# The low-part rotary matmul of the attention scores over all 128 contraction rows

## What is computed

```python
sc = jnp.einsum("bqhd,bkhd->bhqk", q_blk.astype(jnp.float32), k_all) * scale
p = jax.nn.softmax(sc, axis=-1)
```

## Time and profile before

| | us |
|---|---|
| median of 3 runs | 2900.56 |
| lowest and highest | 2898.85, 2903.95 |
| profiled execution, first to last instruction (span) | 2900.2 |
| TensorE busy in it | 2776.2 (96%) |
| VectorE, ScalarE, GpSimd busy | 1664.2, 854.4, 384.8 |

### The profile page before, as it was taken

One profiled execution on the slowest core, in us unless ns is written; L12 is line 12 of the kernel. 1 busy time (PEld: TensorE's weight loads), 2 busy tenths in 40 slices (PEclk: granted clock), 3 DMA queues, 4 the chain that ended last, 5 costly groups with the idle time before them and its releaser, 6 DMA issues.

```text
span 2900.2 us, 31209 instructions
## 1 busy us (share of the span) xinstructions
PE 2776.2 (96%) x11986; PEld 2134.7 (74%) x11986; DVE 1664.2 (57%) x1770; ACT 854.4 (29%) x1102; POOL 384.8 (13%) x266
## 2 busy tenths in 40 slices
PE   6889999999899999999999899999999999999996
PEld 6656777777685888888888766664758888888884
DVE  5635656566526654545444689997275444444455
ACT  2223444444424222222222242224342222222221
POOL 0302122222202440404130010000010000000001
PEclk9989999999998999999999999999989999999998
DMA  6201111111332331313121210110321111111112
GB/s 245 96 17 40 44 40 47 36 51 38 108 112 89 108 109 43 101 58 101 57 81 51 94 73 30 30 43 1 116 77 47 44 58 43 51 51 43 51 41 111
DMA packets 55063, 193.96 MB, mean 67 GB/s; under 512 B 5840, under 2 KB 7120, under 8 KB 54992
## 3 DMA queue, kind: packets, MB, share of 16 engines
q1 hardware_dynamic: 28048, 99.07, 10.5%
q10 hardware_dynamic: 15424, 51.98, 4.7%
q0 software_dynamic: 11520, 41.95, 4.5%
HBM read 172.00 MB, written 20.97 MB: 67 GB/s over the span
## 4 chain that ended last, share of the span: by engine, by line
PE 90%; DVE 4%; issue 3%; ACT 1%; DMA 1%; POOL 0%; ACTq 0%; POOLq 0%; SPq 0%; DVEq 0%
PE psum L1227 25%; PE psum L1229 24%; PE psum L1228 24%; PE psum L1577 4%; PE psum L1439 3%; PE psum L1437 3%; PE psum L1248 2%; PE psum L1449 2%; PE psum L1235 1%; DVE f32r_region L797 1%; PE psum L1281 1%; DMA f_region<-ctx_t 1%; PE psum L1288 1%; PE psum L1424 0%; DVE f_region L801 0%
## 5 line engine op out<-in xcount | busy, mean ns | idle before, releaser
L1227 PE MATMUL psum<-f32r_region 128*128 128x512 f32 (+1 forms) x3288 | 1302.3, 396 | 48.0 <-DVE f32r_region L797 13.2
L1229 PE MATMUL psum<-f32r_region 128*128 128x512 f32 (+1 forms) x3288 | 1273.8, 387 | 0.0
L1228 PE MATMUL psum<-f32r_region 128*128 128x512 f32 (+1 forms) x3288 | 1273.7, 387 | 0.0
L1227 PEld LDWEIGHTS psum<-f32r_region 128*128 128x128 f32 x3288 | 625.8, 190 | 191.1 <-issue 32.8
L1228 PEld LDWEIGHTS psum<-f32r_region 128*128 128x128 f32 x3288 | 626.6, 191 | 126.0 <-issue 6.0
L1229 PEld LDWEIGHTS psum<-f32r_region 128*128 128x128 f32 x3288 | 625.2, 190 | 127.0
L384 ACT ACTIVATE f32r_region<-f_region 128x1024 fp32r<-128x1024 f32 (+1 forms) x251 | 254.4, 1024 | 497.3 <-PE psum L1229 446.9
L1095 DVE SCALAR_TENSOR_TENSOR f_region<-psum,vectors,f_region 128x1023 f32<-128x1023 f32 x88 | 112.8, 1282 | 492.4 <-ACT f_region L673 492.4
L673 ACT ACTIVATE f_region<-psum,vectors 128x1024 f32<-128x1024 f32 x88 | 106.2, 1207 | 589.4 <-PE psum L1229 589.4
L1112 DVE TENSOR_TENSOR f_region<-f_region,psum 128x1024 f32<-128x1024 f32 x160 | 194.8, 1217 | 146.4 <-PE psum L1229 146.4
L347 POOL TENSOR_TENSOR f_region<-f_region,f32r_region_plain 128x512 f32<-128x512 f32 x32 | 52.8, 1649 | 1530.5 <-DVE f_region L1055 1530.5
(11 more groups left out here) (108 smaller groups left out, 1891.1 us busy)
## 6 DMA issues: line engine op xcount, KB each, us to landing
f_region<-units SPq DMA_DIRECT2D x178, 512.0 KB, 3.5
f_region<-mod_w POOLq DMA_DIRECT2D x80, 512.0 KB, 3.9
residual<-f_region ACTq DMA_DIRECT2D x24, 512.0 KB, 4.9
f32r_region_plain<-residual ACTq DMA_DIRECT2D x24, 512.0 KB, 7.7
f32r_region_plain<-mod_w ACTq DMA_DIRECT2D x8, 1024.0 KB, 16.5
f_region<-x_t SPq DMA_DIRECT2D x4, 1024.0 KB, 28.0
heads_out<-f_region ACTq DMA_DIRECT2D x16, 256.0 KB, 2.0
f_region<-heads_out ACTq DMA_DIRECT2D x8, 512.0 KB, 4.3
```

Source lines behind the costliest of these rows:

```text
L1227: pe.matmul(out, wl, xh, start=first, stop=False)
L1228: pe.matmul(out, wh, xl, start=False, stop=False)
L1229: return pe.matmul(out, wh, xh, start=False, stop=last)
```

## The change

The matmul of query high by key low no longer takes rows 0 to 63 of its two operands but all 128. Rows 64 to 127 add the product of query low by key low, which was left out before. Order, tiles, semaphores and columns are the same. In the changed file the last matmul moves up one line, from L1439 to L1438.

```diff
                     three(PS[:, at:at + width], [r(R_Q + p * L + q, P) for p in range(2)],
                           [r(KS[(par // 2) % 2] + p * KEYS + at, width) for p in range(2)], True, False)
 
-                    pe.matmul(PS[:, at:at + width], r(R_Q + 2 * L + q, P)[:ROPE], r(R_KR + KEYS + at, width)[:ROPE],
-                              start=False, stop=False)
+                    pe.matmul(PS[:, at:at + width], r(R_Q + 2 * L + q, P), r(R_KR + KEYS + at, width), start=False, stop=False)
                     mm = pe.matmul(PS[:, at:at + width], r(R_Q + 2 * L + q, P), r(R_KR + at, width), start=False, stop=True)
```

## The result

| | before | after |
|---|---|---|
| median of the runs, us | 2899.7 (4 runs) | 2819.15 (4 runs) |
| lowest and highest, us | 2898.73, 2903.95 | 2816.7, 2822.91 |
| span of the profiled execution, us | 2900.2 | 2819.3 |

The ratio is 0.9717, 95% interval 0.9705 to 0.9729: 2.8% less time. Set against the 2900.56 us from which the prediction started, that is 2818.5 us. Each run of the changed kernel is 1.8 us longer than its span (2821.07 us for the profiled one), so the two profiles compare span with span: 80.9 us.

What follows compares the result with a forecast made beforehand. TensorE was taken to bound the attention scores. From the 2900.2 us span, 76.8 us for row changes came off and 3 us for new waits went back on: 2826.4 us, given as 2826, range 2819 to 2840 us.

Steps and rivals of the forecast that it cites:

- The bound: Attention scores, 197 to 766 us: TensorE sets the time, busy 560.73 of 569 us, VectorE 339.08, ScalarE 223.10.
- The price of a change: Score blocks: about 0.2 us for each switch between 128 and 64 rows, 1.20 us per score step, 76.8 us in all.
- The second way: Idle times before the weight loads of L1437 and L1439, 47.6 + 32.0 = 79.6 us; 80 kept as upper end.
- That a full-height matmul at this place is not stalled: At L1437, 128 rows would fall back to starts 0.23 us apart, so the full 76.8 us is gained.
- the argument from the one-row matmuls: Line 1255: eight one-row matmuls in a row take 1.05 us without stalling, so few rows are not slow in themselves.
- The allowance for new waits: Score steps where VectorE's row maximum comes late: 0 to 12 us of the gain lost, 3 us in the sum.
- VectorE's reserve: VectorE's wait for the scores before the row maximum (L925) falls from 145.5 to about 70 us.
- The clock: Attention stage: mean granted clock read as 0.98 of 2.4 GHz; a microsecond allowed for it in the range.
- VectorE's chain: Rival, score steps: VectorE late by 1.2 us in a quarter to half of 64 steps, 19 to 38 us back; chance 0.06.
- one stall staying: Rival, score blocks: the load of L1439 stays held, half of 76.8 us remains, 2862 us; chance 0.04.
- nothing happening: Rival, score blocks: the hole belongs to the place or the instruction's shape costs nothing, 2900 us; chance 0.03.
- a price by rows: Rival, L1437: the stall grows with rows loaded, 0.2 us for 64 and 0.4 for 128, 2939 us; chance 0.02.

Runs made afterwards that it cites:

- grouped: Kernel before with the three 64-row matmuls of a score step run one after another at its end, not one in each block: 2837.41 us, ratio 0.9782.
- doubled 64-row matmuls: Kernel before with the last matmul of each score block also cut to 64 rows, so two stand in a row: 2900.43 us, ratio 0.9997.
- the late steps: Changed kernel with 64 rows in the low-part rotary matmul in the last 8 of 64 score steps only: 2832.96 us, ratio 0.9759.

## Why the prediction came out as it did

The direction and the mechanism were right. The size was short: 2826 us was forecast, and the median of 2819.15 us is at the lower end of the range, by the ratio (2818.5 us) half a microsecond outside it. That half microsecond is within the noise of the whole time (the interval is 2815 to 2822 us); the stage, which repeats to 0.3 us, shows the errors behind it. Step by step:

- *The bound.* TensorE sets the stage, and 79.7 of the 80.9 us came out of it. Right.
- *The price of a change.* 1.20 us a step from the starts, 76.8 us in all. The score blocks gave 76.6. Right. The second way, 79.6 us of idle time before the loads, agreed by luck. The 129 waits of each load are, but for one, those of the 128 wide blocks, 0.37 and 0.25 us and so 0.62 us a block where the starts give 0.41, and the idle times before the loads of the narrow blocks, 0.14 and 0.13 us or 16.6 us in all, are too short for that view. So 80, the upper end, was no bound.
- *That a full-height matmul at this place is not stalled.* Right, and the argument from the one-row matmuls, that a run of low matmuls is not slow and only the change is, is what the kernels with grouped and with doubled 64-row matmuls showed.
- *The allowance for new waits, 3 us, up to 12.* This step failed: nearly nothing of it came. TensorE's wait for the exponential went from 6.4 to 6.8 us; the steps with a late maximum had their cover, and VectorE's reserve shrank as forecast (70 us, 70.2 measured). The reserve held, but for half a microsecond in one early wait, even with a further 34.7 us taken out of the stage.
- *The clock.* This step failed too, and it is the one that carries the time past the range: without the 3 us for waits, 2900.2 - 76.8 is 2823.4 us, still inside. The sum had no term for the clock and the range gave it one microsecond; what stands in the places with a lowered clock is 4.8 us, or 6.6 by the price of the late steps. The earlier trace rows had it at 0.98 in the stage, which is 11 us of full-speed work in 569, and the prediction took it as given. The places could have been read from the clock by stretches, the first right behind a wait for the exponential.
- *The rivals.* VectorE's chain, one stall staying, nothing happening, and a price by rows are each excluded by a run: the one with the matmul left out, the doubled 64-row, the result itself, and 32 rows.

3 us too many for the waits and 4.8 us too few for the clock are 7.8 us in all; less the 0.6 us by which 64 x 1.19 falls short of 76.8, this is the 7 us between 2826 and 2819. That it closes so well is in part luck: the parts outside the stage, on which the whole time depends too, differ by up to 6 us between profiles of one kernel.

## What to carry to other kernels

Between full-height matmuls, one of 64 or 32 contraction rows is not cheaper for being low: here each crossing cost about 0.2 us at full clock, nearly the 0.23 us of a whole 512-column matmul. If the missing rows can be filled with something harmless or useful, fill them; if not, put the low matmuls next to one another so that the crossings are few. To find such holes, look at the starts of the matmuls and at the weight loads with "issue" before them, since the busy time of TensorE hides both.

## What the runs showed of the hardware

- 96 rows behave as 128 (2821.8 us against 2819.95), 32 as 64 (2904.23 against 2901.29 before).
- The stall at a change of rows costs 1.19 us for six changes in a step at full clock, and 0.33 us for a pair that stands between a 256-column matmul and a transpose. The Trainium skill's "TensorEngine Tiling (Array Packing)", section "Key Properties", says that changing the tiling mode drains TensorE. These traces agree in that the stalls stand where the height goes from 128 to 64 or 32 rows or back, and not between matmuls of one height.
- The granted clock differed with stalls of 0.2 us that TensorE's busy time does not show: over 18 us around the same wait it was 0.50 to 0.72 in the seven profiles with six or more changes in each step there, 0.81 in the one with two, and 0.91 in five of the six without any. In the sixth, with the low-part matmul left out, it was 0.84, by a second wait of 1.11 us shortly ahead.
